# Filler weights and tokens of the recurrence loaded during attention, eight filler units ahead of the first head, masks made later

## The reference, cut to what matters

```python
def forget_gates(z, lb):
    f = lb + (1.0 - lb) * jax.nn.sigmoid(z)
    log_f = jnp.log(jnp.maximum(f, F_MIN))
    k = (1.0 - lb) * jax.nn.sigmoid(-z)
    return k, log_f

# hgrn2_chunk_scan, per chunk: b is the running sum of log_f
o_inter = einsum('bhtk,bhkv->bhtv', qc * exp(b), S)
a = einsum('bhtk,bhsk,bhtsk->bhts', qc, kc, exp(b_t - b_s))   # s <= t
o = o_inter + einsum('bhts,bhsv->bhtv', a, vc)
S = exp(b_last)[..., None] * S + einsum('bhsk,bhsv->bhkv', kc * exp(b_last - b), vc)

# trunk, one layer, for a prompt of 256 tokens and a sample of 1024
x = layer_norm(x, ln_in_g, ln_in_b)
h = x @ w_in[l]
a_out = neighbourhood_attention(q_na, k_na, v_na, na_rpb[l]).reshape(B, T, NA_WIDTH) @ w_branch_na[l]
o_hg = hgrn2_bidirectional(silu(q_hg), i_hg, z_f, z_b, lb_fwd, lb_bwd)
r_out = (rms_norm_heads(o_hg, hg_norm_g[l]) * silu(g_hg)) @ w_branch_hg[l]
mix = sigmoid(gate_na) * a_out + sigmoid(gate_hg) * r_out
x = layer_norm(ALPHA * x + mix @ w_out[l], ln1_g[l], ln1_b[l])
x = layer_norm(ALPHA * x + expert_choice_ffn(x, ...), ln2_g[l], ln2_b[l])
```

## Time and profile before

| | us |
|---|---|
| median of three runs | 3412.97 |
| profiled execution | 3414.22 |
| its span in the trace | 3412.6 |
| TensorE busy | 3056.0 (90%) |
| VectorE busy | 1036.0 (30%) |
| ScalarE busy | 633.2 (19%) |
| GpSimd busy | 440.8 (13%) |

### The profile page before, as it was taken

The page is one execution under the profiler, slowest core; times in us unless marked ns, Lnnn a source line. Parts: engine busy times, 40 slices in busy tenths (PEclk is TensorE's granted clock), DMA queues, the critical chain, the costliest instruction groups (busy, mean ns, idle before and its releaser), DMA issues. The chain is left out here.

```text
span 3412.6 us, 46553 instructions
## 1 busy us (share of the span) xinstructions
PE 3056.0 (90%) x19802; PEld 2824.7 (83%) x19802; DVE 1036.0 (30%) x1609; ACT 633.2 (19%) x1014; POOL 440.8 (13%) x404
## 2 busy tenths in 40 slices
PE   6699997996899959971999999999999999999992
PEld 5578886675778848861999999999999999999992
DVE  6032115765778755647000000000000000000004
ACT  2011114563545333420000000000000000000000
POOL 2220000002434423320000000000000000000002
PEclk9899998998999979985999999999999999999996
DMA  5984522206556353323777777777777777777754
GB/s 208 188 266 148 180 90 55 62 31 239 195 201 208 122 208 125 121 101 136 247 231 244 262 237 247 238 254 240 251 240 241 246 250 247 234 241 262 239 171 143
DMA packets 402148, 669.72 MB, mean 196 GB/s; under 512 B 14250, under 2 KB 201913, under 8 KB 396848
## 3 DMA queue, kind: packets, MB, share of 16 engines
q1 hardware_dynamic: 388496, 619.43, 53.4%
q0 software_dynamic: 12032, 42.33, 5.1%
q10 hardware_dynamic: 1440, 5.24, 0.4%
HBM read 567.63 MB, written 99.32 MB: 195 GB/s over the span
## 5 line engine op out<-in xcount | busy, mean ns | idle before, releaser
L2046 PE MATMUL moe_gate<-moe_xT,pieces_ring 128*128 128x160 f32 x4096 | 580.6, 300 | 0.5 <-DVE moe_xT L2097 0.5
L2046 PE MATMUL moe_up<-moe_xT,pieces_ring 128*128 128x160 f32 x4096 | 577.3, 299 | 0.0
L2046 PEld LDWEIGHTS moe_gate<-moe_xT,pieces_ring 128*128 128x128 f32 x4096 | 563.5, 190 | 1.5 <-DVE moe_xT L2097 0.7
L2046 PEld LDWEIGHTS moe_up<-moe_xT,pieces_ring 128*128 128x128 f32 x4096 | 563.3, 190 | 0.0
L2065 PE MATMUL moe_down<-moe_hdn,pieces_ring 128*128 128x160 f32 x4096 | 561.6, 299 | 0.0
L2065 PEld LDWEIGHTS moe_down<-moe_hdn,pieces_ring 128*128 128x128 f32 x4096 | 557.7, 190 | 0.2
L2106 DVE TENSOR_TENSOR moe_hdn<-moe_sil,moe_up 128x320 f32<-128x320 f32 x128 | 62.5, 488 | 1046.8 <-PE moe_up L2046 984.4
L2082 ACT ACTIVATE moe_sil<-moe_gate 128x320 f32<-128x320 f32 x128 | 56.0, 437 | 1030.3 <-PE moe_gate L2046 1030.3
L1994 POOL DMA_INDIRECT y<-moe_out_p,moe_at_out x16 | 22.5, 1404 | 1603.7 <-DVE moe_out_p L2117 1603.7
L987 POOL TENSOR_TENSOR hg_W<-hg_E 128x640 f32<-128x640 f32 (+1 forms) x92 | 165.5, 1826 | 237.0 <-PE hg_l L1054 106.6
L2117 DVE TENSOR_SCALAR moe_out_s<-moe_turn,main_gates 128x512 f32<-128x512 f32 x32 | 24.0, 751 | 558.4 <-PE moe_turn L2030 558.4
(11 more groups left out here) (221 smaller groups left out, 3923.8 us busy)
## 6 DMA issues: line engine op xcount, KB each, us to landing
pieces_ring<-in_w_gate_e SPq DMA_DIRECT2D x64, 2048.0 KB, 8.1
pieces_ring<-in_w_up_e SPq DMA_DIRECT2D x64, 2048.0 KB, 9.9
pieces_ring<-in_w_down_e SPq DMA_DIRECT2D x64, 2048.0 KB, 8.4
hg_fx<-xs SPq DMA_DIRECT2D x40, 1024.0 KB, 5.4
fr_raw<-in_w_in SPq DMA_DIRECT2D x16, 1024.0 KB, 9.2
ws<-fr_late_split SPq DMA_DIRECT2D x32, 512.0 KB, 3.0
hg_fw<-ws SPq DMA_DIRECT2D x32, 512.0 KB, 7.2
h<-fr_out SPq DMA_DIRECT2D x50, 256.0 KB, 2.9
```

The costliest lines, as they stand in the source:

```text
L2046: last = nc.tensor.matmul(ps[b][:, f, :], weights[:, k, c:c + P], xT[:, w, k, :], start=(k == 0), stop=(k == KD - 1))
```

## The change

Four edits that belong together.

1. `fw` and `fx` with their 13 semaphores move to the stage that owns the bias table, which now lives through the recurrence. SyncE loads the first two tiles and the first 11 blocks in attention's program, behind the load of the fourth pair of heads. The recurrence's program no longer loads them.
2. So that this fits, `qi`, `kiT`, `A` and one half of `fout` are laid into the memory of the bias table.
3. `points` begins with 16 halves instead of 8, so that eight units lead and the list ends four units earlier, after level 2 of head 3. ScalarE evicts units 0 and 1, then takes the logarithms, then evicts units 2 to 5 before `start(0)`, and 6 and 7 after it.
4. The masks are made after the first `prepare` instead of before it.

```diff
+KRING = 11
...
-def stage_attention(nc, ident, h, table, aT):
+def stage_attention(nc, ident, h, table, aT, load_filler):
...
                 with sp.Fori(0, 2) as i:
                     for w in range(2):
                         load(2 * i + w, w, i)
+                load_filler(sp)
                 load(0, 0, 2)
                 sp.wait_ge(loaded[0], 48 * 3)
...
-def stage_recurrence(nc, ident, h, hT, xs, ws, lb_fwd, lb_bwd, o):
+def stage_recurrence(nc, ident, h, hT, xs, ws, lb_fwd, lb_bwd, o, room, fw, fx, fw_in, fx_in):
...
-    SETUP, PER = 6 + 2 * LEVELS + 3, 3 * 2
-    KRING = 11
+    MASKS = 1 + 2 * LEVELS
+    SETUP, PER = 5 + 3 + MASKS, 3 * 2
...
-        qi = s.sb("qi", [P, 2, T])
-        kiT = s.sb("kiT", [P, 2, NT, P])
+        qi = room[:, 0:2 * T].rearrange("p (d t) -> p d t", d=2)
+        kiT = room[:, 2 * T:4 * T].rearrange("p (d c t) -> p d c t", d=2, c=NT)
...
-        A = s.sb("A", [P, T])
+        A = room[:, 4 * T:5 * T]
...
-        fw = s.sb("fw", [P, KRING, 2, SLAB], F32R)
-        fx = s.sb("fx", [P, 2, 2, KD, P], F32R)
-        fout = s.sb("fout", [P, 2, SLAB])
+        fout = [room[:, 5 * T:5 * T + SLAB], s.sb("fout", [P, SLAB])[:]]
...
-        points = [("first",)] * 8
+        points = [("first",)] * 16
...
                 load_head(0)
-                load_tile(0)
-                for n in range(KD):
-                    load_block(n)
-                load_tile(1)
                 load_head(1)
-                for n in range(KD, KRING):
-                    load_block(n)
...
                 gates(0, 0)
+                evict(2)
+                logarithms(0)
                 evict(units_until(("first",)) - 2)
-                logarithms(0)
                 start(0)
                 evict(units_until(("first",)))
...
-                dve.wait_ge(chain, SETUP)
+                dve.wait_ge(chain, SETUP - MASKS)
+
+                def masks():
+
+                    step = Steps(MASKS)
+                    step.base = SETUP - MASKS + PER
+                    dve.wait_ge(iota_done, 2)
+                    nc.vector.tensor_tensor(xor_i, cols_i, rows_i, ALU.bitwise_xor).then_inc(chain, 1)
...
                 prepare(0, 0)
+                masks()
                 run_sums(0)
...
+            fw, fx = b.sb("fw", [P, KRING, 2, SLAB], F32R), b.sb("fx", [P, 2, 2, KD, P], F32R)
+            fw_in, fx_in = b.sems("fw_in", KRING), b.sems("fx_in", 2)
+
+            def load_filler(sp):
+                for i in range(2):
+                    sp.dma_start(fx[:, i].bitcast(F32), xs[i]).then_inc(fx_in[i], 16)
+                for n in range(KRING):
+                    sp.dma_start(fw[:, n].bitcast(F32), ws[n // KD, n % KD]).then_inc(fw_in[n], 16)
+
+            stage_attention(nc, ident, h, table, aT, load_filler)
+            stage_recurrence(nc, ident, h, hT, xs, ws, lb_fwd, lb_bwd, o, table[:].rearrange("p h n c -> p (h n c)"),
+                             fw, fx, fw_in, fx_in)
```

More of the change, by code:

```diff
@@ L844, in stage_recurrence @@
              "a_done", "ds_mm", "s_made", "o_mm", "o_copied", "stored", "chain", "lb_ready"))
-        fw_in, fx_in, fx_half = s.sems("fw_in", KRING), s.sems("fx_in", 2), s.sem("fx_half")
+        fx_half = s.sem("fx_half")
         f_copied, f_stored = s.sem("f_copied"), s.sems("f_stored", 2)
@@ L924, in load_block @@
                 def load_block(n):
-                    if n >= KRING:
-                        sp.wait_ge(fx_half, last_half(n - KRING) + 1)
+                    sp.wait_ge(fx_half, last_half(n - KRING) + 1)
                     sp.dma_start(fw[:, n % KRING].bitcast(F32), ws[n // KD, n % KD]).then_inc(fw_in[n % KRING], 16)
@@ L934, in load_tile @@
                 def load_tile(i):
-                    if i >= 2:
-                        sp.wait_ge(fx_half, 2 * (i - 1))
+                    sp.wait_ge(fx_half, 2 * (i - 1))
                     sp.dma_start(fx[:, i % 2].bitcast(F32), xs[i % NT]).then_inc(fx_in[i % 2], 16)
@@ L941, in store_unit @@
                     at = LATER[i // NT] * SLAB
-                    sp.dma_start(h[i % NT * P:(i % NT + 1) * P, at:at + SLAB], fout[:, i % 2])\
+                    sp.dma_start(h[i % NT * P:(i % NT + 1) * P, at:at + SLAB], fout[i % 2])\
                       .then_inc(f_stored[i % 2], 16)
@@ L946, in store_head @@
                     sp.wait_ge(o_copied, (hd + 1) * NG)
-                    sp.dma_start(o[:, hd * P:(hd + 1) * P].rearrange("(t p) c -> p t c", p=P), chunked(A[:]))\
+                    sp.dma_start(o[:, hd * P:(hd + 1) * P].rearrange("(t p) c -> p t c", p=P), chunked(A))\
                       .then_inc(stored, 16)
@@ L1113, in evict @@
                             act.wait_ge(f_stored[i % 2], 16 * (i // 2))
-                        nc.scalar.activation(fout[:, i % 2], f_acc[i % 2][:], ACT.Copy).then_inc(f_copied, 1)
+                        nc.scalar.activation(fout[i % 2], f_acc[i % 2][:], ACT.Copy).then_inc(f_copied, 1)
                 act.wait_ge(chain, 1)
@@ L1205, in _ @@
                 step.next()
[L1207 to L1216, removed]
                 for d in range(2):
@@ L1221, in _ @@
                 step.next()
-                dve.wait_ge(chain, SETUP)
+                dve.wait_ge(chain, SETUP - MASKS)
[4 more added lines that the diff above has]
+                    nc.vector.tensor_tensor(xor_i, cols_i, rows_i, ALU.bitwise_xor).then_inc(chain, 1)
+                    dve.wait_ge(chain, step.next())
+                    for n in range(LEVELS):
+                        m = P >> (n + 1)
+                        nc.vector.tensor_scalar(below, xor_i, 2.0 * m, None, ALU.is_lt).then_inc(chain, 1)
+                        dve.wait_ge(chain, step.next())
+                        nc.vector.scalar_tensor_tensor(mask[:, n, :], xor_i, float(m), below, ALU.is_ge, ALU.mult)\
+                          .then_inc(chain, 1)
+                        dve.wait_ge(chain, step.next())
                 def prepare(p, w):
                     count_of = Steps(PER)
-                    count_of.base = SETUP + p * PER
+                    count_of.base = SETUP + p * PER if p else SETUP - MASKS
                     for d in range(2):
@@ L2234, in build @@
                             table[:].rearrange("p h n c -> p (h n c)"), on_pool)
-            stage_attention(nc, ident, h, table, aT)
-        stage_recurrence(nc, ident, h, hT, xs, ws, lb_fwd, lb_bwd, o)
+            fw, fx = b.sb("fw", [P, KRING, 2, SLAB], F32R), b.sb("fx", [P, 2, 2, KD, P], F32R)
[8 more added lines that the diff above has]
+                             fw, fx, fw_in, fx_in)
         gates = [s.sb(f"gates{n}", [CAPS[n], NE]) for n in range(2)]
```

## The result

| | median us | runs | range |
|---|---|---|---|
| before | 3412.97 | 7 | 3410.28 to 3415.44 |
| changed | 3423.81 | 7 | 3422.91 to 3432.18 |

The changed kernel takes 1.0036 times as long (95% interval 1.0024 to 1.0048), 10.8 us more. The forecast of 3412.4 and its range, which ended at 3420.0, missed it. The profiled execution took 3432.18 us (span 3430.5), the slowest of the seven, so its stretches overstate the loss: it is 17.9 us longer in its span than the profiled execution before, where the medians differ by 10.8.

The account below looks back on a forecast made before the run. It took TensorE, busy 90% of the span, to bound the kernel, and transfers to bound the lead. Terms 0 + 1.9 + 0 + 0.75 + 0.3 - 3.5 = -0.55 us gave 3412.4 us, range 3404.5 to 3420.

Parts of the forecast that it names:

- Middle heads: Heads 0 to 2: slab loads move from levels 5 and 6 to 1 and 2; +0.3 us, bounds 0 to +4.
- Filler loaded in attention: Attention: thirteen DMAs, 7.9 MB, hide in a 44 us hole; cost 0, bounds -0.5 to +3 us.
- The lead: Before head 0: eight units instead of four, with unit 2 waiting for tile 2; head 0 starts 1.9 us later.
- ScalarE's order and the masks: Before head 0: reordered evictions and logarithms, and later masks, stay hidden; cost 0.
- One more release: After the recurrence: a further semaphore clearing and barrier; +0.75 us, bounds 0 to +1.5.
- Head 3: Last head: four filler units leave levels 3 to 6; -3.5 us, bounds -9 to +1.
- the clock paragraph: Head 3: TensorE pauses lower its clock, pairs 4 to 7 take 4.6 us; gain shrinks from -4.8 to -3.1.
- (a): Lead and head 3: tail gains in full, lead's pause is short; -9 us, 3404; 13%.
- (b): Lead: tile 2 stuck behind both `v` transfers; landing at 807 makes the whole +9.5 us, 3422; 12%.
- (c): Head 3's end: clock stays low, output products cost 4 us more; whole +4, 3417; 11%.
- (d): Attention or slab changes: loads don't hide, or stall at three transitions; +4 to +7 us, 3417 to 3420; 4%.

Follow-up runs that it names:

- a_om: The changed kernel with the masks back at their old place, ahead of the first clamps; 3422.49 us, 1.0037 times before.
- noreload: The changed kernel without any reload of filler weights, all four slabs using the first one's blocks (for measuring only); 3410.08 us, 1.0001 times before.
- l8om: The changed kernel with eight halves ahead of the first head instead of sixteen and the masks at their old place; 3393.57 us, 0.9951 times before.
- before16: The kernel before with sixteen half units ahead of the first head instead of eight, nothing preloaded; 3447.95 us, 1.0107 times before.
- five_warm: The kernel five plus idle TensorE matmuls ahead of the pair products of levels 4 to 7 of head 3; 3416.11 us, 1.0016 times before.
- five: The changed kernel, but at a slab change SyncE loads five blocks, the next tile, then three spare blocks; 3412.05 us, 1.0004 times before.

## Why the prediction was wrong, step by step

- **Middle heads, +0.3, bounds 0 to +4: this step failed.** It measured +13.0 in the profiled execution and +9.8 in a_om's. I had seen that the slab's change moves from levels 5 and 6 to 1 and 2 and priced one block, the fifth. I did not follow the queue behind it: three spare blocks and then the tile. The same queue ran before, but it fell where TensorE waits for VectorE anyway, 1.36 us at 893.56 and 6.31 us at 998.60. An estimate was at hand: 4.2 + 1.05 MB at 406 GB/s take 12.9 us, where a tile alone landed in 5.4, with TensorE filled all the while. It would have been low, but have given the warning: from the first block's issue to the tile's use it was 18.2 us both times, because the last four blocks wait until the unit before is done and other loads and stores share the engines (7.0 and 6.5 MB moved, at 386 and 356 GB/s). Of that the levels took up a part, and the waits were 3.06 and 5.47 us. Against noreload head 1 lost 7.6 us, which is the wait and some 2 us of matmuls at half clock behind it (0.53 from 981.75 to 986.00). Head 0 lost 6.0 us in this execution and 3.2 in a_om's. The difference is mostly level 7, where pairs took 4.61 us here and 2.47 in a_om, behind pauses of 3.24 and 3.22 us. Why the clock fell there in the one and not in the other stays open.
- **Filler loaded in attention, 0: right.** The loads lie in the hole: 670 to 714 moved 162 GB/s, not 0, with TensorE busy 42.22 us of 44 in both. The stage began 2.6 us later than before in this execution, but at 769.9 to 776.4 us in the ten other kernels with the preload and at 773.1 and 776.3 in the two without, so no cost in attention can be seen.

```profile
670.00:714.00 44.00, 42.22 (x270) 31.87 (x271) 28.69 (x71) 26.81 (x66) 0.00 (x0) 1.00 0.40 162
```

- **The lead, +1.9: right.** It measured +2.6 in the profiled execution and +2.3 in a_om. Unit 2 started 21.6 us into the stage; forecast were 20.75. Units 2 to 7 took 35.6 us; forecast were 35.7.
- **ScalarE's order and the masks, 0: right for sixteen halves.** For the masks a_om shows it; with eight halves their place is worth 6 us of lead (l8om). ScalarE's new order cost nothing, as forecast. What the old order would have cost with eight units the prediction doesn't say; in before16 it let TensorE wait 6.89 us.
- **One more release, +0.75: smaller.** The release of line 103 starts with a drain on SyncE, and there are now eleven of them, where there were ten. From the barrier's event to the next stage's first work it is 1.2 us, not the 0.75 of before. The further release costs the difference, +0.4, and not another 0.75.

```profile
L103 SPq DRAIN  x11: 7/7/7, 2.1 to 3430.0; - x11
...
L908 SPq EVENT_SEMAPHORE  x1: 17/17/17, 1223.1 to 1223.1; - x1
...
1224.28 1.28 ACT L1572 ACT_TABLE_LOAD   x1 [5.26 <-PEq L103]
```

- **Head 3, -3.5: about right.** Up to the outputs it gained 1.5 us in the profiled execution; the whole rest, release included, 1.2 us there, 3.4 in a_om, 3.6 in five. So the size is met in a_om and five, and less than half of it in the profiled execution. The pair products came as laid out but for the last. The forecast put the ends of VectorE's products of rounds 5 to 8 at 43.0, 50.4, 55.7 and 60.1 us into the head; the pairs that use them, 4 to 7, began at 44.8, 49.9, 55.1 and 62.8:

```profile
1189.82 4.45 PE L1046 MATMUL hg_l<-hg_W 128*128 128x128 f32 x20 [7.11 <-DVE bias_table L1281]
...
1194.98 2.47 PE L1046 MATMUL hg_l<-hg_W 128*128 128x128 f32 x20 [0.71 <-DVE bias_table L1281]
...
1200.14 4.00 PE L1046 MATMUL hg_l<-hg_W 128*128 128x128 f32 x20 [2.69 <-DVE bias_table L1281]
...
1207.83 4.00 PE L1046 MATMUL hg_l<-hg_W 128*128 128x128 f32 x20 [3.68 <-DVE bias_table L1281]
```

Pairs 4 are at half clock behind a pause of 7.11 us, as the clock paragraph said. The Trainium skill says in TensorE: Matmul & The Clock Gate (Part 1) that the throttled state is the default and activity lifts it; the trace agrees, with 4.45 and 4.00 us behind pauses against 2.39 where filler runs ahead. That the clock would decide the time of head 3 was not borne out (five_warm).

- **The rivals.** (a) didn't occur, because the lead and the tail were as forecast. (b) named a stuck tile, but in the lead; tile 2 came as forecast. (c) didn't occur: the output products began with 0.49 us and went on at 0.39, as before. (d) had the mechanism, slab loads that stall at each of three changes, at 4% and 4 to 7 us. It was the case at two of the three, with 10 to 13 us. A rival that is priced by a guess at the end of a list deserved the arithmetic above.

## What to carry to other kernels

When work is moved along a hand-written order, everything that is tied to its count moves with it; here a reload of 4.2 MB every tenth unit. Ask for each such event whether its new place is one where the bound engine waits anyway, and add up the queue it stands in, down to the last transfer that someone waits for. Load in an idle stretch what the next stage needs first, but take the gain as an earlier start: filler moved ahead costs most of its time there (18 of 22 us for four units) and gives back only what the levels it leaves can use (6 us).

## What the runs showed of the hardware that was not expected

When GpSimd's differences and VectorE's operations ran side by side, now the one, now the other was slowed. In round 8 of head 3, first in the changed kernel, then in five:

```profile
1194.42 7.27 POOL L979 TENSOR_TENSOR hg_W<-hg_E 128x640 f32<-128x640 f32 x3 [6.05 <-PE hg_l L1046]
...
1195.66 0.82 DVE L1251 TENSOR_TENSOR hg_W<-hg_E 128x640 f32<-128x640 f32 x1
...
1196.40 1.48 DVE L1257 TENSOR_TENSOR hg_W<-hg_W,hg_qT 128x1280 f32<-128x1280 f32 x1
```

```profile
1175.47 4.26 POOL L981 TENSOR_TENSOR hg_W<-hg_E 128x640 f32<-128x640 f32 x3 [5.94 <-PE hg_l L1048]
...
1176.83 1.79 DVE L1253 TENSOR_TENSOR hg_W<-hg_E 128x640 f32<-128x640 f32 x1
...
1178.54 2.54 DVE L1259 TENSOR_TENSOR hg_W<-hg_W,hg_qT 128x1280 f32<-128x1280 f32 x1
```

In the changed kernel GpSimd took 7.27 us and VectorE's difference and product 0.82 and 1.48; in five it was 4.26 against 1.79 and 2.54, with the same instructions. In the changed kernel that delayed the last exponential, and pairs 7 waited 3.68 us. In a_om, whose program for head 3 is that of the changed kernel, GpSimd took 5.55 us there, so it is not fixed by the program. What decides who gives way stays open.
